# The normed operand h moved by 32 bytes in its SBUF partitions

## The chip, the core and the metric

The kernel runs on one core of a Trainium2 chip. The metric is the device time of one launch in microseconds (us). Below, the SBUF address of a tensor means its byte address within each of the 128 partitions; it is the same in all of them.

## What is computed

The reference passes a 256 x 1024 activation `x` through two blocks of two layers each, all in float32. Cut to what matters here:

```python
for l in range(2):                                # first block
    x = x + 0.5 * swiglu_ffn(rmsnorm(x, ffn1_norm[l]), ffn1_w_up[l], ffn1_w_down[l])
    x = x + mixer(rmsnorm(x, mix_norm[l]), w_in[l], ...)      # windowed attention + 31-tap conv
    x = x + 0.5 * swiglu_ffn(rmsnorm(x, ffn2_norm[l]), ffn2_w_up[l], ffn2_w_down[l])
    x = rmsnorm(x, final_norm[l])
for i in range(2):                                # second block, modulated by c
    h = rms_norm(x, norm_mix_pre[i]) * (1.0 + sc_m) + sh_m
    y = mixer_ab(h, ...) if i == 0 else mixer_c(h, ...)       # recurrence + sparse attention; short conv
    x = x + (1.0 + g_m) * rms_norm(y, norm_mix_post[i])
    h = rms_norm(x, norm_ffn_pre[i]) * (1.0 + sc_f) + sh_f
    y = conv_ffn(h, ...)
    x = x + (1.0 + g_f) * rms_norm(y, norm_ffn_post[i])
```

So nearly all the work is products of a normed activation `h` (1024 channels, 256 tokens) with weight matrices, and, in the four-plus-two feed-forward layers, of a hidden tile with the down projection.

## The kernel before

**Split products.** Every float32 weight and every float32 operand is split in two fp32r parts, a high part and a low one, and each product is made of three matmuls: high x high, high weight x low operand, low weight x high operand. `product` writes them:

```python
mm(o, w_hi[:, n, at], hi, first, False, share=share)
mm(o, w_hi[:, n, at], lo, False, False, share=share)
mm(o, w_lo[:, n, at], hi, False, last, sig, share)
```

The first operand is stationary (128 x 128, put in by a weight load), the second one moves (128 x 256). All matmuls go through the helper on line 522, so all have that line in the profile.

**Weights.** There are 663 weight tiles of 128 x 1024 floats (512 KB). SP's queue loads each into one of six `w_raw` slots; ScalarE copies it to `w_hi` (line 1053), VectorE subtracts to make `w_lo` (line 1477), each in one of three slots. A tile serves 24 matmuls, for eight blocks of 128 along the contraction.

**The operands.** `h_hi` and `h_lo` hold the normed activation as eight blocks of 256 tokens. ScalarE writes `h_hi` (lines 1083, 1097, 1243, 1383) and VectorE `h_lo` (lines 1505, 1567, 1807, 1818, 2079, 2092). They are the moving operand in `column`, `column_pair`, `normed_pair` and `late_pair`, and the stationary one in `token_product` (there a slice of `w_hi` or `w_lo` moves). `hid_hi` and `hid_lo` hold the hidden tile of a feed-forward layer, two buffers each; `spare_operands` holds four more tiles. In `late_pair` and the columns after it, one column's 24 matmuls take `hid` for two blocks, `spare_operands` for two and `h` for four, all added up in the same half of a PSUM bank.

**A feed-forward step** (132 of them, line 1591 on) is two columns of 24 matmuls with `h` moving, into the two halves of a bank, and then the `down` product, 24 matmuls with `hid` moving, each block into another bank half. TensorE's program, and so the order of work, is written out by hand; other engines follow it by semaphores.

**Where the tensors lie.** `sb` reserves SBUF tensors one behind the other, each rounded up to 32 bytes. Addresses in the built programs:

| tensor | bytes | before | after | before, mod 64 | after, mod 64 |
|---|---|---|---|---|---|
| `work` | 8192 | 24704 | 24704 | 0 | 0 |
| `w_hi` | 12288 | 58496 | 58496 | 0 | 0 |
| `w_lo` | 12288 | 70784 | 70784 | 0 | 0 |
| `h_hi` | 8192 | 83072 | 83104 | 0 | 32 |
| `h_lo` | 8192 | 91264 | 91296 | 0 | 32 |
| `vecs` | 5696 | 99456 | 99520 | 0 | 0 |
| `tabs` | 13980 | 105152 | 105216 | 0 | 0 |
| `gate_a` | 2048 | 119136 | 119200 | 32 | 32 |
| `hid_hi` | 2304 | 121184 | 121248 | 32 | 32 |
| `hid_lo` | 2304 | 123488 | 123552 | 32 | 32 |
| `spare_operands` | 4096 | 125792 | 125856 | 32 | 32 |
| `arena` | 78880 | 149952 | 150016 | 0 | 0 |

Every block of `w`, `h`, `hid` and `spare_operands` is a multiple of 512 bytes long, so each block has its tensor's remainder. Before the change `w_hi`, `w_lo`, `h_hi` and `h_lo` lie at multiples of 128 bytes, and `hid_hi`, `hid_lo` and `spare_operands` 96 bytes past one.

Of the kernel before, what the change touches and what calls it, by code (L numbers as in the profile page):

```python
# [193 lines left out]
def build(nc, x_in, weights, vecs_in, tables_in, bv_in, mod_in, out):  # L194
    with ExitStack() as ctx:
        def sb(name, *shape, dt=F32):
            return ctx.enter_context(nc.sbuf_tensor(name, [P, *shape], dt))
# [9 lines left out]
        w_raw = sb("w_raw", RAW, TILE)  # L207
        w_hi = sb("w_hi", SPLIT, TILE, dt=F32R)
        w_lo = sb("w_lo", SPLIT, TILE, dt=F32R)
        h_hi = sb("h_hi", KT, SEQ, dt=F32R)  # L210
        h_lo = sb("h_lo", KT, SEQ, dt=F32R)
        vecs = sb("vecs", N_VEC)
        tabs = sb("tabs", N_TAB)
        gate_a = sb("gate_a", 2, SEQ)
# [2097 lines left out]
```

## Time and profile before

| | |
|---|---|
| time, median of 3 runs | 2372.85 us (2372.59 to 2374.2) |
| time of the profiled execution | 2372.82 us |
| its span, first to last instruction | 2371.0 us |
| mean granted TensorE clock | 0.982 |
| TensorE matmuls | 18598, 98% of the span |
| weight loads | 18598, 95% |
| VectorE | 2844, 73% |
| ScalarE | 1739, 50% |
| HBM read | 403.07 MB, 170 GB/s over the span |

Busy time of a matmul is from its start to its modelled end, and matmuls overlap, so 98% says that the engine always has one in flight, and not how fast they follow each other. That pace is read from the starts in the timeline. The profiled execution took 1.8 us more than its span.

### The profile page before, as it was taken

The page shows a single profiled execution, that of the slowest core. Times are in us where ns is not written, and L with a number is a line of the kernel's source. Part 1 is how long each engine was busy: PE and PEld are TensorE (multiplying, and loading weights), DVE is VectorE, ACT ScalarE, POOL GpSimd, SP SyncE. Part 2 cuts the span into 40 slices and gives each one's busy share as a digit, 9 for nine tenths or more (in the row PEclk, how much of TensorE's full clock was granted, in tenths as well). Part 3 has the DMA queues.
Part 4 walks back from the last instruction along what each step waited for, and adds up shares of the span by engine and source line. Part 5 has one row for each costly group of instructions (what it writes and reads, how often), then busy time and mean ns, then how long its engine had stood idle before and what let it go on. Part 6 is the DMA issues. An engine that isn't in the chain of part 4 may idle for free.

```text
span 2371.0 us, 46678 instructions
## 1 busy us (share of the span) xinstructions
PE 2316.3 (98%) x18598; PEld 2259.9 (95%) x18598; DVE 1731.8 (73%) x2844; ACT 1179.2 (50%) x1739; POOL 98.5 (4%) x196
## 2 busy tenths in 40 slices
PE   8999999999999999999999999999999999999998
PEld 8999999999999999999999999989888999999997
DVE  6667899868667866899976766777445766667766
ACT  4335444565444444554455544446454565435564
POOL 0000020000000000022000000000000000000000
PEclk9999999999999999999999999999699999999999
DMA  8775555235775776565415677443122455353552
GB/s 310 235 242 189 184 167 170 87 126 198 248 243 197 267 239 230 166 182 174 143 55 194 233 238 239 143 151 117 44 72 72 159 180 183 125 169 125 181 182 97
DMA packets 114082, 412.31 MB, mean 174 GB/s; under 512 B 13984, under 2 KB 14112, under 8 KB 113696
## 3 DMA queue, kind: packets, MB, share of 16 engines
q1 hardware_dynamic: 96768, 352.26, 44.5%
q0 software_dynamic: 16896, 56.64, 7.8%
q8 instruction: 94, 1.54, 0.3%
q10 hardware_dynamic: 288, 1.57, 0.2%
q14 instruction: 36, 0.29, 0.0%
HBM read 403.07 MB, written 1.05 MB: 170 GB/s over the span
## 4 chain that ended last, share of the span: by engine, by line
PE 91%; DVE 6%; ACT 2%; issue 1%; DMA 0%; DVEq 0%; SPq 0%; ACTq 0%
PE bank L522 90%; PE bank L707 1%; DVE arena L1680 1%; DVE w_lo L1477 1%; DVE rinv L1513 0%; ACT w_hi L1053 0%; ACT arena L1362 0%; DMA vecs<-vectors 0%; DVE arena L1799 0%; DVE mod_w_buf L1762 0%; DVE arena L2066 0%; DVE work L2055 0%; DVE rinv L1796 0%; DVE mod_w_buf L2048 0%; ACT rinv L1076 0%
## 5 line engine op out<-in xcount | busy, mean ns | idle before, releaser
L522 PE MATMUL bank<-h_hi,w_hi 128*128 128x256 f32 x3840 | 1095.0, 287 | 12.6 <-ACT h_hi L1083 4.0
L522 PE MATMUL bank<-h_hi,w_lo 128*128 128x256 f32 x3840 | 1082.4, 283 | 0.0
L522 PE MATMUL bank<-h_lo,w_hi 128*128 128x256 f32 x3840 | 1069.2, 284 | 0.1
L1477 DVE TENSOR_TENSOR w_lo<-w_raw,w_hi 128x1024 fp32r<-128x1024 f32 x663 | 807.9, 1222 | 335.2 <-ACT w_hi L1053 329.8
L1053 ACT ACTIVATE w_hi<-w_raw 128x1024 fp32r<-128x1024 f32 x663 | 699.6, 1057 | 612.5 <-PE bank L522 611.9
L522 PEld LDWEIGHTS bank<-h_hi,w_hi 128*128 128x128 f32 x3840 | 738.4, 192 | 26.9 <-issue 15.8
L522 PEld LDWEIGHTS bank<-h_hi,w_lo 128*128 128x128 f32 x3840 | 738.6, 192 | 0.0
L522 PEld LDWEIGHTS bank<-h_lo,w_hi 128*128 128x128 f32 x3840 | 729.9, 192 | 3.7 <-DVE h_lo L1505 2.2
L522 PE MATMUL bank<-hid_hi,w_hi 128*128 128x256 f32 (+1 forms) x1168 | 332.8, 285 | 9.8 <-DVE w_lo L1477 2.8
L522 PE MATMUL bank<-hid_lo,w_hi 128*128 128x256 f32 (+1 forms) x1168 | 330.3, 283 | 0.0
L522 PE MATMUL bank<-hid_hi,w_lo 128*128 128x256 f32 (+1 forms) x1168 | 330.0, 283 | 0.0
L522 PEld LDWEIGHTS bank<-hid_hi,w_hi 128*128 128x128 f32 x1168 | 222.7, 191 | 13.2 <-issue 9.4
L522 PEld LDWEIGHTS bank<-hid_hi,w_lo 128*128 128x128 f32 x1168 | 223.5, 191 | 0.0
L522 PEld LDWEIGHTS bank<-hid_lo,w_hi 128*128 128x128 f32 x1168 | 223.3, 191 | 0.0
L1680 DVE SCALAR_TENSOR_TENSOR arena<-arena,vecs 128x256 f32<-128x256 f32 x520 | 215.1, 478 | 0.0
L522 PE MATMUL bank<-arena 128*128 128x64 f32 (+3 forms) x640 | 111.3, 320 | 3.2 <-DVE arena L2002 1.7
L1858 DVE SCALAR_TENSOR_TENSOR mod_w_buf<-mod_w_buf,c_act 128x1024 f32<-128x1024 f32 x84 | 107.5, 1279 | 1.5 <-DMA mod_w_buf<-mod_w 1.2
L1591 DVE TENSOR_TENSOR hid_hi<-gate_a,bank 128x256 fp32r<-128x256 f32 x132 | 55.3, 419 | 69.3 <-ACT gate_a L1130 68.8
L522 PEld LDWEIGHTS bank<-arena 64*128 64x128 f32 (+1 forms) x640 | 92.3, 206 | 12.4 <-DVE work L2031 1.9
L500 POOL DMA_DIRECT2D mod_w_buf<-mod_w x96 | 51.1, 533 | 1072.7 <-DVE mod_w_buf L1858 537.6
L1130 ACT ACTIVATE gate_a<-bank 128x256 f32<-128x256 f32 x88 | 34.0, 386 | 114.4 <-PE bank L522 114.4
L522 PE MATMUL bank<-w_hi,h_hi 128*128 128x256 f32 (+1 forms) x240 | 69.0, 288 | 2.1 <-DVE arena L1751 1.4
(248 smaller groups left out, 2074.2 us busy)
## 6 DMA issues: line engine op xcount, KB each, us to landing
w_raw<-weights SPq DMA_DIRECT2D x663, 512.0 KB, 3.4
mod_w_buf<-mod_w POOLq DMA_DIRECT2D x96, 512.0 KB, 4.8
mod_w_buf<-arena POOLq DMA_DIRECT2D x96, 64.0 KB, 3.6
tabs<-shape_tables SPq DMA_DIRECT2D x1, 1682.0 KB, 14.1
work<-v_bias ACTq DMA_DIRECT2D x2, 768.0 KB, 4.4
x<-x_fm SPq DMA_DIRECT2D x1, 1024.0 KB, 5.1
out_fm<-x SPq DMA_DIRECT2D x4, 256.0 KB, 2.2
vecs<-vectors SPq DMA_DIRECT2D x1, 708.0 KB, 10.5
```

The costliest lines, as they stand in the source:

```text
L500: pool.dma_start(mod_w[:, n % MOD_BUF, :], mod_in[n]).then_inc(mod_w_full[n % MOD_BUF], 16)
L522: ins = pe.matmul(o, lhs, rhs, start=start, stop=stop, skip_group_check=share)
L707: ins = pe.transpose(o, src, tab("identity"))
L1053: act_f(w_hi[:, n % SPLIT, :], w_raw[:, n % RAW, :], ACT.Copy).then_inc(hi_ready, 1)
L1130: act_f(gate_a[:, par, :], half(UP + par, 0), ACT.Silu).then_inc(gate_ready, 1)
L1477: v.tensor_tensor(w_lo[:, n % SPLIT, :], w_raw[:, n % RAW, :], w_hi[:, n % SPLIT, :].bitcast(F32), ALU.subtract).then_inc(lo_ready[n % SPL ...
L1591: v.tensor_tensor(hid_hi[:, par, :], g, half(b, 1), ALU.mult)
L1680: ins = v.scalar_tensor_tensor(dst[:, m, :], src[:, m, k:k + SEQ], tap, dst[:, m, :], ALU.mult, ALU.add)
L1858: ins = v.scalar_tensor_tensor(o, src, c, o, ALU.mult, ALU.add)
```

## The change

Eight floats (32 bytes) are reserved ahead of `h_hi`, and eight behind `h_lo`. Nothing reads or writes them. `h_hi` and `h_lo` move by 32 bytes, and all that is reserved behind them by 64. No instruction is added, taken out or moved on any engine; the two programs differ in the line numbers (by 2 behind the change) and in addresses.

```diff
         w_raw = sb("w_raw", RAW, TILE)
         w_hi = sb("w_hi", SPLIT, TILE, dt=F32R)
         w_lo = sb("w_lo", SPLIT, TILE, dt=F32R)
+        sb("half_line", 8)
         h_hi = sb("h_hi", KT, SEQ, dt=F32R)
         h_lo = sb("h_lo", KT, SEQ, dt=F32R)
+        sb("other_half_line", 8)
         vecs = sb("vecs", N_VEC)
         tabs = sb("tabs", N_TAB)
```

## Rows read from the trace of the kernel before

**Rows 1.** The page: span, busy time (share of span) and instructions of each engine, chain's shares.

```profile
span 2371.0 us, 46678 instructions
PE 2316.3 (98%) x18598; PEld 2259.9 (95%) x18598; DVE 1731.8 (73%) x2844; ACT 1179.2 (50%) x1739; POOL 98.5 (4%) x196
...
PE 91%; DVE 6%; ACT 2%; issue 1%; DMA 0%; DVEq 0%; SPq 0%; ACTq 0%
```

**Rows 2.** Groups of TensorE: count, busy us, mean ns of one, idle us before.

```profile
L522 PE MATMUL bank<-h_hi,w_hi 128*128 128x256 f32 x3840 | 1095.0, 287 | 12.6 <-ACT h_hi L1083 4.0 <-DVE w_lo L1477 3.5 <-DVE h_lo L1567 3.2
L522 PE MATMUL bank<-h_hi,w_lo 128*128 128x256 f32 x3840 | 1082.4, 283 | 0.0
L522 PE MATMUL bank<-h_lo,w_hi 128*128 128x256 f32 x3840 | 1069.2, 284 | 0.1
L522 PE MATMUL bank<-hid_hi,w_hi 128*128 128x256 f32 (+1 forms) x1168 | 332.8, 285 | 9.8 <-DVE w_lo L1477 2.8 <-DVE hid_lo L1928 2.5 <-DVE hid_lo L1594 2.4
...
L522 PE MATMUL bank<-w_hi,h_hi 128*128 128x256 f32 (+1 forms) x240 | 69.0, 288 | 2.1 <-DVE arena L1751 1.4 <-DVE w_lo L1477 0.7
```

**Rows 3.** Tile h_lo on TensorE, 230 to 268 us: ns min/median/max; first, last start.

```profile
L522 PE MATMUL bank<-h_lo,w_hi x106: 283/283/283, 229.8 to 267.6; 128*128 128x256 f32 x106
```

**Rows 4.** Timeline of one feed-forward step on TensorE: start us, us, instruction.

```profile
124.55 0.28 PE L522 MATMUL bank<-h_hi,w_hi 128*128 128x256 f32 x1
...
125.61 0.28 PE L522 MATMUL bank<-h_hi,w_hi 128*128 128x256 f32 x1
...
130.29 0.28 PE L522 MATMUL bank<-hid_hi,w_hi 128*128 128x256 f32 x1
...
130.53 0.28 PE L522 MATMUL bank<-hid_hi,w_lo 128*128 128x256 f32 x1
...
133.14 0.28 PE L522 MATMUL bank<-h_hi,w_hi 128*128 128x256 f32 x1
```

**Rows 5.** Timeline of one column that takes hid, spare_operands and then h.

```profile
542.86 0.28 PE L522 MATMUL bank<-hid_hi,w_hi 128*128 128x256 f32 x1
...
544.28 0.28 PE L522 MATMUL bank<-h_hi,w_hi 128*128 128x256 f32 x1
544.39 0.28 PE L522 MATMUL bank<-h_lo,w_hi 128*128 128x256 f32 x1
...
545.71 0.28 PE L522 MATMUL bank<-hid_hi,w_hi 128*128 128x256 f32 x1
```

**Rows 6.** Tiles hid_lo (130.3 to 133.1 us) and spare_operands (whole span) on TensorE.

```profile
L522 PE MATMUL bank<-hid_lo,w_hi x8: 277/280/285, 130.4 to 132.9; 128*128 128x256 f32 x8
...
L522 PE MATMUL bank<-spare_operands,w_hi x128: 277/281/285, 500.3 to 1299.6; 128*128 128x256 f32 x128
```

**Rows 7.** Groups of VectorE and ScalarE, shapes apart, that write a split part.

```profile
L1594 DVE TENSOR_TENSOR hid_lo<-gate_a,hid_hi 128x256 fp32r<-128x256 f32 x132 | 56.1, 425 | 4.5
...
L1807 DVE TENSOR_TENSOR h_lo<-work,h_hi 128x256 fp32r<-128x256 f32 x16 | 6.1, 422 | 3.6 <-ACT h_hi L1243 3.2
...
L1083 ACT ACTIVATE h_hi<-work 128x256 fp32r<-128x256 f32 x40 | 15.9, 418 | 9.4 <-DVE work L1518 9.4
```

**Rows 8.** Line 1680, the convolution's taps, and line 1277: ns min/median/max.

```profile
L1680 DVE SCALAR_TENSOR_TENSOR arena<-arena,vecs x520: 470/478/487, 241.8 to 2121.6; 128x256 f32<-128x256 f32 x174
...
L1277 ACT ACTIVATE hid_hi<-arena x8: 400/414/419, 1590.8 to 1605.9; 128x256 fp32r<-128x256 f32 x8
```

**Rows 9.** Windows: us, busy (count) of PE, PEld, DVE, ACT, POOL; clock, DMA, GB/s.

```profile
300.00:360.00 60.00, 60.00 (x556) 57.69 (x551) 57.71 (x102) 27.64 (x53) 15.42 (x32) 1.00 0.55 172
360.00:380.00 20.00, 18.93 (x170) 18.05 (x169) 19.40 (x38) 7.75 (x12) 3.06 (x6) 1.00 0.53 175
380.00:408.00 28.00, 28.00 (x224) 27.09 (x223) 28.00 (x53) 10.76 (x13) 0.00 (x0) 1.00 0.56 186
```

**Rows 10.** Cores: span and mean granted TensorE clock.

```profile
core 0: 2371.0 us, clock 0.982
```

## The prediction

> **What bounds the kernel now.** I read the page first. TensorE has a matmul in flight for 98% of the span, and 91% of the chain that ended last is TensorE [rows 1]. The groups of TensorE say which matmuls: three groups of 3840 have `h` moving, 11,520 of 18,598, and their idle time before them is 12.6, 0.0 and 0.1 us [rows 2]. So they hardly wait; the time is their number times the pace at which they follow each other, and the mean duration of 283 to 287 ns is not that pace, since they overlap.
>
> The pace is in the starts. Between 229.8 and 267.6 us there are 106 matmuls of `h_lo`, every third one of an unbroken run: 37.8 us over 105 gaps of three matmuls is 120.0 ns per matmul, and all 106 durations are 283 ns [rows 3]. The stream with `h` moving is locked to one rhythm.
>
> The same trace has matmuls that already lie as the change will put `h`: `hid_hi`, `hid_lo` and `spare_operands` are at 32 mod 64, with the same shape, type and stationary tiles. In a feed-forward step the 22 gaps from 130.53 to 133.14 us, `hid` moving, take 2.61 us, 118.6 ns each; in the same step the 39 gaps from 125.61 to 130.29 us, with `h` moving, take 4.68 us, 120.0 ns [rows 4]. That could come from the bank that `down` changes with each block. The column that takes both kinds excludes it: twelve matmuls of `hid` and `spare_operands` start from 542.86 to 544.28 us, 1.42 us or 118.3 ns each; then, in the same half bank with the same weight tile, come twelve of `h`, of which the last eleven take 545.71 - 544.39 = 1.32 us, 120.0 ns [rows 5]. Durations say the same: `hid_lo` and `spare_operands` spread over 277 to 285 ns with medians of 280 and 281, where `h_lo` has 283 throughout [rows 3, 6]. The position of the moving operand, or where it stands to the weights, is worth about 1.5 ns per matmul. I take 118.5 ns as the pace off a multiple of 64, between 118.3 and 118.6.
>
> **The change part by part.** It adds no instruction and no wait. Five things could change.
>
> *Matmuls with `h` moving.* In the feed-forward layers a gain is already there in part: the first nine matmuls after `hid` still run fast, 124.55 to 125.61 us, 117.8 ns each, before the stream locks [rows 4]. So I cost whole steps. One is 133.14 - 124.55 = 8.59 us for 72 matmuls; at 118.5 ns it would be 8.53. That is 0.06 us, for 132 steps (as many as line 1594 has rows, [rows 7]) 7.9 us. The steps hold 132 x 48 = 6,336 matmuls with `h`; the other 5,184 lose 120.0 - 118.5 = 1.5 ns each, 7.8 us. Together 15.7 us.
>
> *What of it can't be banked.* The mean clock is 0.982 [rows 10]. If that is time at 1.2 in place of 2.4 GHz, (1 - 0.982) x 2 x 2371 = 85 us, 3.6% of the span, ran at the lower level; there a matmul of 256 columns takes about twice as long, and I expect no gain: -0.6 us. And in each of the first block's two mixers VectorE is the tighter engine for a while: busy 57.71 of 60 us, 19.40 of 20 and 28.00 of 28 [rows 9]. A faster TensorE gains nothing where VectorE makes the next `w_lo` late. From 360 to 380 us TensorE has 170 matmuls, of which I take 150 as `h` moving: 150 x 1.5 ns = 0.2 us, twice 0.4 us. From 300 to 360 us there are 60 / 0.120 = 500, so 0.75 us per mixer and 1.5 us in both; VectorE has 2.3 us idle of 60 there, so I count half as lost, 0.8 us. Together -1.2 us. What is late next there is VectorE's own work, the taps and the low parts.
>
> *Matmuls with `h` stationary.* These are 3 x 240 = 720 [rows 2]; `h` moves off and the moving weight slice stays on a multiple of 64. No row shows a stationary operand off such a multiple beside a 256-column fp32r one on it. If what counts is how the two stand to each other, they gain 1.5 ns each, 1.1 us, less the 384 in windows where VectorE is busy all the time (192 per mixer, the third window): 336 x 1.5 = 0.5 us. If only the moving operand counts, nothing. I take 0.3 us and keep -0.7 (1 ns worse each) to +0.5.
>
> *VectorE and ScalarE on `h`.* VectorE writes `hid_lo`, off a multiple of 64, in 425 ns and `h_lo`, on it, in 422; ScalarE writes `hid_hi` in 414 (median) and `h_hi` in 418 [rows 7, 8]. The 31 taps read the same row at starts 4 bytes apart, and all 520 lie between 470 and 487 ns with a median of 478 [rows 8]. So the shift costs these engines nothing: at most 3 ns for each of some 124 writes of `h_lo`, 0.4 us, mostly in the norms where TensorE waits. I take 0.
>
> *All that lies behind `h`, moved by 64 bytes.* Remainders to 64 stay. Remainders to 128 change: `hid` and `spare_operands` go from 96 to 32. Before, the moving operand that is off stands 32 bytes below a multiple of 128, and the weights on one; after, all stand 32 above. No row shows that. I take the pace of 118.5 for both, since both leave 32 when divided by 64; the third rival prices the doubt.
>
> **The sum.** 15.7 - 0.6 - 1.2 + 0.3 = 14.2 us less. The profiled execution took 2372.82 us, 0.03 from the median, so the time is 2372.8 - 14.2 = 2358.6 us, 0.60% less. Its own range: with 118.3 ns and all banked, 132 x (8.59 - 8.52) + 5,184 x 1.7 ns + 0.5 = 9.2 + 8.8 + 0.5 = 18.5 us, 2354; with 118.8 and the same losses doubled, 132 x 0.04 + 5,184 x 1.2 ns - 3.6 - 0.7 = 5.3 + 6.2 - 4.3 = 7.2 us, 2366.
>
> **The rivals.** *Nothing changes.* The spread of `hid` could come from something else that sets it apart, such as its distance from the weights (`h` lies right behind `w_lo`, `hid` 22 KB beyond `h`), or the fast rhythm could be one that falls to 120.0 in runs longer than the 24 matmuls of `down`; the first nine of `h` in a step do run fast and then lock. For it: the change keeps that distance. Against it: in the column of [rows 5] the stream takes up 120.0 one matmul after `h` comes, and 118.6 holds through all of `down`. The time would be 2372.8.
> The Trainium skill speaks for this rival. "TensorE: Matmul & The Clock Gate", Part 2, says of the two read ports that loading the next tile's weights takes no SBUF bandwidth from the running matmul; "SBUF — State Buffer", on Door 1, gives SBUF lines of 16 bytes, to which a shift by 32 changes nothing. By both the time stays at 2372.8. The trace agrees with neither as the whole story, since equal matmuls differ by 1.5 ns with no other difference that I can name than where they lie.
>
> *A bigger gain.* With `h` off, no part of a run falls back to 120.0, and the whole stream could settle at the quick end of what `hid` shows: 277 ns against 283 [rows 6] is 6 ns; half of it on 11,520 matmuls is 34.6 us, 2338. For it: durations do reach it. Against it: the mean pace over 22 matmuls is 118.6, so quick ones are paid for by slow ones.
>
> *Slower.* The place is `product` itself, at the third of these remainders: with every moving operand 32 bytes above the weights' multiple of 128, each matmul could meet the weight load once more, where 32 bytes below it met it less. The slow end of `hid` is 285 ns, 2 ns over `h` [rows 6]: 11,520 x 2 = 23.0 us, and the 3,504 of `hid` [rows 2] would go from 118.5 to 122.0, 12.3 us; together 35 us, 2408. It decides from 120.0 ns on for `h`, if `hid` keeps its pace; if `hid` goes along, all at 119.7 is even (11,520 x 0.3 = 3,504 x 1.2, roughly, without the fast starts). A 256-column operand of 1,024 bytes off a multiple of 64 also touches 17 stretches of 64 bytes and not 16, which would speak for slower; `hid` has that too and is faster.
>
> **How the numbers follow.** The forecast has 0.64, no change 0.14, the bigger gain 0.06, slower 0.16. A measurement of this kernel tells about 0.2%, 4.7 us, from no change. All of the forecast's own range, 2354 to 2366, is beyond that, so faster has 0.64 + 0.06 = 0.70; of the slower case 0.01 is within the bound, which makes same 0.15 and slower 0.15. The range for 8 in 10 takes in the forecast and no change: 2352 to 2375.
>
> **What would show it.** In the changed kernel's trace, a run with only `h` moving such as 230 to 268 us should have starts 118.5 ns apart and durations that spread from 277 to 285 ns; a feed-forward step should take 8.53 us; `h_lo`'s writes and the taps should stay at 422 and 478 ns; VectorE should be busy for all of the token pairs of both first mixers, and these should take as long as before. The forecast is wrong if `h` still runs at 120.0, or if `hid` leaves 118.5.

## The result and the profile after

The changed kernel takes 2342.66 us (median of 4 runs, 2339.43 to 2342.86), the kernel before 2373.11 on the same chip: a ratio of 0.9868, 95% interval [0.9851, 0.9885], so 30 us or 1.3% faster. The forecast was 14.2 us, with a range that ended at 2352. Direction and place were right, and the size was half of what came.

The page of the changed kernel, in the lines that answer to [rows 1]:

```profile
span 2337.6 us, 46678 instructions
PE 2280.9 (98%) x18598; PEld 2222.3 (95%) x18598; DVE 1729.4 (74%) x2844; ACT 1180.0 (50%) x1739; POOL 98.2 (4%) x196
...
PE 91%; DVE 6%; ACT 2%; issue 1%; DMA 0%; DVEq 0%; SPq 0%; ACTq 0%
```

The span, of the fastest of the four runs, is 33.4 us shorter with the same instructions and the same shares in the chain. Its groups of TensorE (count, busy us, mean ns, idle before; compare [rows 2]):

```profile
L524 PE MATMUL bank<-h_hi,w_hi 128*128 128x256 f32 x3840 | 1082.3, 284 | 13.7 <-DVE w_lo L1479 4.0 <-ACT h_hi L1085 4.0 <-DVE h_lo L1569 3.2
L524 PE MATMUL bank<-h_hi,w_lo 128*128 128x256 f32 x3840 | 1069.6, 280 | 0.0
L524 PE MATMUL bank<-h_lo,w_hi 128*128 128x256 f32 x3840 | 1057.7, 281 | 0.1
L524 PE MATMUL bank<-hid_hi,w_hi 128*128 128x256 f32 (+1 forms) x1168 | 329.6, 282 | 10.3 <-DVE w_lo L1479 3.0 <-DVE hid_lo L1930 2.5 <-DVE hid_lo L1596 2.4
```

`h` lost 3 ns in mean duration, and `hid`, which the forecast had as unchanged, lost 3 too (285 to 282). Idle time before each group rose by about 1 us at most: no engine took TensorE's place as the bound. The tile `h_lo` on TensorE between 230 and 268 us (count, ns min/median/max, first and last start; compare [rows 3]):

```profile
L524 PE MATMUL bank<-h_lo,w_hi x108: 277/280/281, 230.0 to 267.9; 128*128 128x256 f32 x108
```

37.9 us over 107 gaps of three is 118.1 ns per matmul, where it was 120.0, and the durations are no longer all alike. Two feed-forward steps from the timeline (start us, us, instruction), the first from the first layer, the second from the layer at 600 us; compare [rows 4]:

```profile
132.02 0.28 PE L524 MATMUL bank<-h_hi,w_hi 128*128 128x256 f32 x1
...
137.67 0.28 PE L524 MATMUL bank<-hid_hi,w_hi 128*128 128x256 f32 x1
...
140.50 0.28 PE L524 MATMUL bank<-h_hi,w_hi 128*128 128x256 f32 x1
...
606.25 0.28 PE L524 MATMUL bank<-h_hi,w_hi 128*128 128x256 f32 x1
...
611.85 0.28 PE L524 MATMUL bank<-hid_hi,w_hi 128*128 128x256 f32 x1
...
614.65 0.28 PE L524 MATMUL bank<-h_hi,w_hi 128*128 128x256 f32 x1
```

The first takes 8.48 us (117.8 ns a matmul), the second 8.40 (116.7): before, every steady step took 8.59. In the second, `h` and `hid` both run at 116.7 ns. About two thirds of the steps of this trace take 8.40 and one third 8.48, each for whole stretches of a layer; that is 132 x 0.16 = 21 us of the 33.4. The other 12 us lie outside the steps. Matched start by start in the two traces, the 5,184 matmuls with `h` there gain 2.9 ns each where they follow without a wait (15 us), and late operands take 3.5 us of it back.

Groups of VectorE and ScalarE, then line 1682 (the taps), and the windows of [rows 9]:

```profile
L1596 DVE TENSOR_TENSOR hid_lo<-gate_a,hid_hi 128x256 fp32r<-128x256 f32 x132 | 56.1, 425 | 4.5
...
L1809 DVE TENSOR_TENSOR h_lo<-work,h_hi 128x256 fp32r<-128x256 f32 x16 | 6.1, 422 | 3.6 <-ACT h_hi L1245 3.2
...
L1085 ACT ACTIVATE h_hi<-work 128x256 fp32r<-128x256 f32 x40 | 15.9, 420 | 9.4 <-DVE work L1520 9.4
...
L1682 DVE SCALAR_TENSOR_TENSOR arena<-arena,vecs x520: 464/477/485, 238.9 to 2091.0; 128x256 f32<-128x256 f32 x174
...
300.00:360.00 60.00, 60.00 (x558) 57.87 (x557) 58.57 (x102) 30.10 (x56) 16.30 (x34) 1.00 0.57 172
360.00:380.00 20.00, 18.82 (x169) 17.86 (x168) 19.74 (x39) 5.46 (x6) 0.47 (x1) 1.00 0.53 180
380.00:408.00 28.00, 28.00 (x226) 26.94 (x224) 28.00 (x55) 13.07 (x18) 0.00 (x0) 1.00 0.51 171
```

The other engines take what they took, and VectorE is as tight as before in the first block's mixers.

### The profile page after: what moved, and what is told of

Its sections match the earlier page's. It is cut to its first block, busy times and chain, and to the rows that moved or that the text cites. A ratio compares the mean times of both kernels' runs of the same rounds, so it can differ in the third digit from the quotient of the medians.

```text
span 2337.6 us, 46678 instructions
## 1 busy us (share of the span) xinstructions
PE 2280.9 (98%) x18598; PEld 2222.3 (95%) x18598; DVE 1729.4 (74%) x2844; ACT 1180.0 (50%) x1739; POOL 98.2 (4%) x196
## 4 chain that ended last, share of the span: by engine, by line
PE 91%; DVE 6%; ACT 2%; issue 1%; DMA 0%; DVEq 0%; SPq 0%; ACTq 0%
PE bank L524 90%; PE bank L709 1%; DVE w_lo L1479 1%; DVE arena L1682 1%; DVE rinv L1515 0%; ACT w_hi L1055 0%; DMA vecs<-vectors 0%; DVE arena L1801 0%; ACT arena L1364 0%; DVE mod_w_buf L1764 0%; DVE arena L2068 0%; DVE rinv L1798 0%; DVE work L2057 0%; ACT rinv L1078 0%; ACT arena L1312 0%
## 5 line engine op out<-in xcount | busy, mean ns | idle before, releaser
L524 PE MATMUL bank<-h_hi,w_hi 128*128 128x256 f32 x3840 | 1082.3, 284 | 13.7 <-DVE w_lo L1479 4.0
L524 PE MATMUL bank<-h_hi,w_lo 128*128 128x256 f32 x3840 | 1069.6, 280 | 0.0
L524 PE MATMUL bank<-h_lo,w_hi 128*128 128x256 f32 x3840 | 1057.7, 281 | 0.1
L524 PEld LDWEIGHTS bank<-h_hi,w_hi 128*128 128x128 f32 x3840 | 725.8, 189 | 28.8 <-issue 17.4
L524 PEld LDWEIGHTS bank<-h_hi,w_lo 128*128 128x128 f32 x3840 | 725.8, 189 | 0.0
L524 PEld LDWEIGHTS bank<-h_lo,w_hi 128*128 128x128 f32 x3840 | 717.2, 189 | 4.6 <-DVE h_lo L1507 2.7
```

The source lines that it names most:

```text
L524: ins = pe.matmul(o, lhs, rhs, start=start, stop=stop, skip_group_check=share)
```

## The experiments

From here on the **distance** of an operand is the address of the moving tensor less that of the weights, modulo 256. Within each tensor the blocks are multiples of 512 bytes apart, and so are `w_hi` and `w_lo`, so each moving tensor has one distance. Before the change `h` has 0, `hid` and `spare_operands` 224; after it all three have 32. In each kernel only reserved bytes differ, unless said otherwise. "Step" is one feed-forward step near 600 us, with the pace of its 48 matmuls with `h` and its 24 with `hid`; starts are read to 0.01 us, so these paces are good to some 0.2 and 0.4 ns. Each run has one trace. Ratios are to the kernel before, with 95% intervals.

| run | h | hid | time, us | ratio | step, us | h ns | hid ns |
|---|---|---|---|---|---|---|---|
| before | 0 | 224 | 2373.11 | 1 | 8.59 | 119.6 | 118.8 |
| changed | 32 | 32 | 2342.66 | 0.9868 [0.9851, 0.9885] | 8.40 | 116.7 | 116.7 |
| e1 | 32 | 96 | 2353.66 | 0.9917 [0.99, 0.9933] | 8.54 | 118.1 | 119.6 |
| e2 | 0 | 32 | 2371.94 | 0.9994 [0.9984, 1.0003] | 8.59 | 120.0 | 117.9 |
| e3 | 64 | 96 | 2355.4 | 0.9926 [0.9909, 0.9942] | 8.54 | 117.9 | 120.0 |
| e4 | 96 | 96 | 2383.49 | 1.0039 [1.0025, 1.0053] | 8.64 | 120.0 | 120.0 |
| e5 (weights and h moved) | 0 | 64 | 2374.02 | 1.0002 [0.9993, 1.0012] | 8.59 | 120.0 | 117.9 |
| e6 (weights by 32, h by 128) | 96 | 64 | 2372.34 | 0.9994 [0.9985, 1.0004] | 8.58 | 120.0 | 117.5 |
| e7 (h_hi 16, h_lo 144) | 16/144 | 224 | 2352.34 | 0.9916 [0.99, 0.9933] | 8.49 | 117.7 | 118.3 |
| e8 (h_hi 32, h_lo 128) | 32/128 | 96 | 2358.58 | 0.9939 [0.9923, 0.9956] | 8.53 | 117.9 | 119.6 |
| e9 (step near 2222 us) | 64 | 64 | 2347.84 | 0.9896 [0.9879, 0.9912] | 8.48 | 117.7 | 117.9 |
| e10 | 32 | 64 | 2333.63 | 0.9829 [0.9812, 0.9845] | 8.33 | 116.9 | 113.3 |
| e11 | 160 | 160 | 2354.77 | 0.9915 [0.9898, 0.9931] | 8.45 | 117.3 | 117.5 |
| e12 (weights moved too) | 32 | 32 | 2340.16 | 0.9862 [0.9846, 0.9879] | 8.48 | 117.9 | 117.5 |
| e13 | 192 | 192 | 2304.46 | 0.9718 [0.9702, 0.9734] | 8.17 | 113.3 | 113.8 |
| e15 (288, 32 to 512) | 32 | 32 | 2339.92 | 0.9858 [0.9841, 0.9874] | 8.40 | 116.7 | 116.7 |
| e16 | 32 | 224 | 2344.81 | 0.9874 [0.9856, 0.9891] | 8.45 | 116.9 | 118.3 |
| e17 | 128 | 128 | 2363.4 | 0.9959 [0.9944, 0.9973] | 8.54 | 118.8 | 118.3 |
| e18 | 224 | 224 | 2358.23 | 0.9937 [0.992, 0.9954] | 8.52 | 118.3 | 118.3 |

Several traces hold steps of more than one length, each for stretches of a layer: 8.40 and 8.48 us in the changed kernel, e12 and e15; 8.47 and 8.53 in e1; 8.33 and 8.43 in e10; 8.45, 8.54 and 8.64 in e11; 8.16 and 8.48 in e9, e13 and e14. The steady steps of the other kernels agree within 0.05 us. The row shows the one near 600 us. A pace that a stretch keeps is called its rhythm below.

**First question: which part of the change gave it?** The expectations of the first runs count remainders to 128 and call 224 "96"; that was too coarse, and e1, e3 and e4 moved `hid` from 224 to 96 without my meaning to (e7 and e8 have the same flaw in `h_lo`, below).

e1 moves `h` by 32 and what lies behind by 128:

```diff
+        sb("pad_before_h", 8)
         h_hi = sb("h_hi", KT, SEQ, dt=F32R)
         h_lo = sb("h_lo", KT, SEQ, dt=F32R)
+        sb("pad_behind_h", 24)
```

> h_hi and h_lo 32 bytes on as in the change, but 96 bytes behind them in place of 32, so that all that lies behind keeps its remainder to 128 (hid and spare_operands 96). Theory A, the remainders to 128 of moving and stationary operand decide together: h runs at 117.0 ns a matmul as after the change, hid goes back to about 118.4 (it had 118.6 before); 3504 matmuls x 1.4 ns = 5 us over the changed kernel, about 2347. Theory B, only being off a multiple of 64 counts and hid ran slower before because it came out of locked runs of h: h and hid both at 117.0, about 2342.

Measured 2353.66 us, 11 more than the changed kernel where theory A had 5: `hid`, now at 96, runs at 119.6 ns and not at 118.4, and `h` at 118.1 where the changed kernel has 116.7. Theory B is out.

e2 leaves `h` and moves all behind it by 64 bytes (`+ sb("pad_behind_h", 16)` behind `h_lo`).

> h stays where it was (a multiple of 128); only what lies behind it moves by 64 bytes, so hid and spare_operands go from remainder 96 to 32. Theory A: h keeps 120.0 ns, hid goes from 118.4 to 117.0, about 2373 - 5 = 2368. Theory B: no remainder to 64 changes, so nothing does: 2373.

Measured 0.9994, no difference. Its timeline shows why theory A's 5 us did not come:

```profile
602.94 0.28 PE L523 MATMUL bank<-h_hi,w_hi 128*128 128x256 f32 x1
...
608.70 0.28 PE L523 MATMUL bank<-hid_hi,w_hi 128*128 128x256 f32 x1
...
611.53 0.28 PE L523 MATMUL bank<-h_hi,w_hi 128*128 128x256 f32 x1
```

`hid` is quicker (2.83 us for 24, where it took 2.85), but the 48 matmuls with `h` now take 5.76 us, 120.0 ns each, where they took 5.74: most of the quick start that they had after `hid` at 224 [rows 4] is gone. The step stays at 8.59 us. So moving the rest is worth nothing alone; beside a moved `h` it counts, as e1 shows.

e3 (`h` by 64) and e4 (`h` by 96), both with what lies behind moved by 128: 16 and 16 floats reserved for e3, 24 and 8 for e4.

> h 64 bytes on: a multiple of 64, not of 128; what lies behind moves by 128 and keeps its remainders. Theory A (remainder to 128): h leaves 120.0 ns for another pace, and I can't say which; hid keeps 118.4. Theory B (remainder to 64): h stays at 120.0, 2373.

> h 96 bytes on (where hid is, 96 mod 128), what lies behind keeps its remainders. Theory A: h runs as hid did before, about 118.5 ns, 1.5 ns less on 11520 matmuls, 2373 - 15 = 2358, which is what the prediction had. Theory B: 117.0 as after the change, 2342.

e3, `h` on a multiple of 64, is 0.7% faster; theory B predicted no change. e4, `h` off it as in the change, is 0.4% slower than the kernel before:

```profile
607.35 0.29 PE L524 MATMUL bank<-h_hi,w_hi 128*128 128x256 f32 x1
...
613.11 0.29 PE L524 MATMUL bank<-hid_hi,w_hi 128*128 128x256 f32 x1
...
615.99 0.29 PE L524 MATMUL bank<-h_hi,w_hi 128*128 128x256 f32 x1
```

All 72 matmuls of the step take 8.64 us, 120.0 ns each. Being on or off a multiple of 64 bytes is not what counts.

**Second question: the operand's own place, or its distance from the weights?** e5 moves weights and `h` by 32; e6 moves the weights by 32 and `h` by 128, so that `h` keeps its remainder to 128 (both edits in one, the remarks are mine):

```diff
+        sb("pad_before_w", 8)
         w_hi = sb("w_hi", SPLIT, TILE, dt=F32R)
         w_lo = sb("w_lo", SPLIT, TILE, dt=F32R)
+        sb("pad_before_h", 24)         # e6 only
         h_hi = sb("h_hi", KT, SEQ, dt=F32R)
         h_lo = sb("h_lo", KT, SEQ, dt=F32R)
+        sb("pad_behind_h", 24)         # e5 only
```

> w_hi, w_lo and h all 32 bytes on (remainder 32 to 128), the rest keeps its remainders (hid 96). Theory R, what counts is where the moving operand stands to the stationary one: h is 0 bytes from the weights again and runs at 120.0 ns, hid stands 64 from them; about 2370. Theory M, what counts is the moving operand's own remainder: h at 117.3 ns as with h alone moved, about 2354.

> only w_hi and w_lo 32 bytes on; h on a multiple of 128 and hid at 96 as before. Theory R: h stands 32 below the weights, as with h at 96, and runs at 120.0 ns with durations that spread; hid stands 64 above, about 117.7 ns; some 5 us either side of 2373. Theory M: h keeps 120.0 ns with all durations alike, hid 118.4, 2373 as before.

In e5 `h` lies where the change put it, 32 off, and runs as in the kernel before: the tile `h_lo`, 230 to 260 us,

```profile
L524 PE MATMUL bank<-h_lo,w_hi x84: 283/283/283, 229.8 to 259.7; 128*128 128x256 f32 x84
```

29.9 us over 83 gaps of three, 120.1 ns, all durations alike, and 1.0002 in time. Weights and `h` both moved against `x`, `work` and `w_raw`, so where they lie against those counts for nothing here. In e6 `h` is on a multiple of 128 as before, and the time of 0.9994 fits both theories. Its durations spread over 281 to 285 ns where they had been 283 throughout, and `hid`, whose remainder to 128 stayed, takes 117.5 ns where it took 118.4, close to e5, which has it at the same distance of 64. `h` takes 120.0 in the steps, which both theories had. e12 moves weights by 32 and the operands by 64, so distance 32 with `h` on a multiple of 64:

> weights at 32, all moving operands at 64, so on a multiple of 64 bytes but 32 from the weights. Theory R (distance to the stationary operand): 2342 as the changed kernel, 116.7 ns. Theory M (the moving operand's own remainder): as with all at 64, 2346 or more; the shifted weights are also written by ScalarE and VectorE, which should cost nothing.

Measured 0.9862, the changed kernel's 0.9868 within both intervals, and its steps take 8.40 or 8.48 us, as there. e5 and e12 decide it and e6 agrees in its paces: the distance counts, and the own remainder to 64 or 128 does not (theory R).

**Third question: finer, and for each part of h?** e7 takes `h_hi` and `h_lo` as slices that begin 4 floats into rooms of 32 floats more; e8 reserves 8 floats ahead of `h_hi` and 24 between the two.

```diff
-        h_hi = sb("h_hi", KT, SEQ, dt=F32R)
-        h_lo = sb("h_lo", KT, SEQ, dt=F32R)
+        h_room = [sb(name, KT * SEQ + 32, dt=F32R)[:, 4:4 + KT * SEQ] for name in ("h_hi", "h_lo")]
+        h_hi, h_lo = (r.rearrange("p (k t) -> p k t", k=KT) for r in h_room)
```

> h_hi and h_lo 16 bytes on, the rest keeps its remainders. If stretches of 16 bytes are what the engine fetches by (the rule that the prediction set beside its first rival), 16 is as good as 32: 117.3 ns and 2354. If the pace follows the distance in finer steps or only in steps of 32, h stands between 0 and 32: 117.3 to 120.0 ns, 2354 to 2373.

> h_hi 32 bytes on, h_lo where it was, the rest keeps its remainders. If each matmul's pace follows its own operand, two of three matmuls run at 117.3 and the third at 120.0 ns, 118.2 on average: about 2373 - 13 = 2360. If the stream locks as a whole, it is 120.0 or 117.3 throughout: 2373 or 2354.

Neither edit does what its expectation says. A room of 32 floats more is 128 bytes, so in e7 `h_hi` has a distance of 16 and `h_lo` one of 144; in e8 the 8 and 24 floats put `h_lo` at 128 and not at 0. To 128 bytes, as I then counted, both were as meant. e7 gives 0.9916, less than e16's 0.9874 with all of `h` at 32 and `hid` also at 224; what 16 bytes alone are worth, no run shows. e8's 2358.58 is near the 2360 that it was expected to have with `h_lo` at 0, but that is luck: nothing lay at 0. Its `h` runs at 117.9 ns, where e1 with all of `h` at 32 has 118.1 or less and e17 with all at 128 has 118.8; whether each matmul follows its own operand is not shown by that.

**Fourth question: how many bytes does the distance count to?** Floats reserved ahead of `h` and behind it: e9 16 and 8, e10 8 and 16, e11 40 and 8, e15 72 and 8, e17 32 and 8, e13 48 and 8.

> h, hid and spare_operands all 64 bytes from the weights (to 128). If the pace follows the distance, all run at the 117.7 ns that h had at 64 with hid at 96: 132 steps x 72 x (119.3 - 117.7) ns + 5184 x 2.3 ns = 27 us less, 2346. If only being off a multiple of 64 gives the full gain, this stays near 2373, or at 2355 as with h at 64 alone.

> h 32 bytes from the weights, hid and spare_operands 64. If what matters is that no operand stands at 0 or 96, about as the changed kernel: 2342 to 2346. If the full gain needs all moving operands at one distance, it stays near 2353, as with hid at 96.

> h, hid and spare_operands 160 bytes from the weights to 256, so 32 to 128. If the distance counts to 128 bytes, 2342 as the changed kernel and 116.7 ns in a feed-forward step; if to 256 or more, another time.

> h 288 bytes from the weights (32 to 256, 288 to 512), hid and spare_operands 32 to 512: both as in the changed kernel to 256, and exchanged to 512. If the distance to 256 decides, 2342 as the changed kernel, 117.0 ns for both; if more than 256 bytes count, another time.

> h, hid and spare_operands 128 bytes from the weights, which fills the gap in the row 0, 32, 64, 96, 160, 192, 224. If 128 is to the two streams what 0 is, 120.0 ns and about 2383; if the good distances are 64 and 192 and the row has a period of 128 in the main, 120.0 as well; if 0 alone locks at 120.0, about 118 ns and 2350.

32 and 160 differ (0.9868 and 0.9915, disjoint intervals), and so do 96 and 224 (1.0039 and 0.9937; every steady step takes 8.64 and 8.52 us): 128 bytes are too few. 32 and 288 agree (0.9868 and 0.9858): 256 do, as far as these runs go. 128 is neither as 0 nor as 64; its 0.9959 was in none of my expectations. e10 beat its expectation of 2342 to 2346 by 8 us.

> h, hid and spare_operands 192 bytes above the weights (to 256), that is 64 below. So far, by the distance to 256: 0 gave 120.0 ns a matmul, 16 117.8, 32 117.0, 64 117.7, 96 119.9, 160 117.9, 224 118.4, and the 240 full-width token products, where the weights move 192 above h, 116.1. If the distance to 256 decides, about 117 ns and 2343 to 2355. If the distance to 128 did, 117.7 as at 64, 2348.

At 192 the kernel takes 2304.46 us, 2.8% less than before and 1.6% less than the changed one, and no expectation of mine had it. `h` lies on a multiple of 64 there. A step:

```profile
572.91 0.28 PE L524 MATMUL bank<-h_hi,w_hi 128*128 128x256 f32 x1
...
578.35 0.28 PE L524 MATMUL bank<-hid_hi,w_hi 128*128 128x256 f32 x1
...
581.08 0.28 PE L524 MATMUL bank<-h_hi,w_hi 128*128 128x256 f32 x1
```

8.17 us, 113.5 ns a matmul. This is the fastest version found. Its four times spread from 2298.9 to 2309.52 us, and the trace is that of the fastest.

**Fifth question: was the forecast's proxy sound?** e16 gives `h` 32 and keeps `hid` at 224 (8 floats ahead, 56 behind); e18 puts `h` at `hid`'s 224 (56 and 8).

> the change's part on h alone, done cleanly: h 32 bytes from the weights, all that lies behind moved by 256, so that hid and spare_operands keep the distance of 224 to 256 that they had before (in the earlier run with h at 32 they went from 224 to 96). If each operand's pace follows its own distance to 256, h at 117.0 to 117.3 and hid at 118.4 ns: 3504 x 1.4 ns = 5 us over the changed kernel, 2347. If hid at 224 was only fast in the wake of h at 0, hid at 119.6 and 2353.

> h 224 bytes from the weights, just where hid stood before, and hid and spare_operands kept at 224. This is the kernel that the prediction's proxy speaks of. If the pace belongs to the distance, all moving operands run at 118.4 ns as hid did: 132 x (8.59 - 8.52) us + 5184 x 1.6 ns = 17 us less, 2356, the time that the prediction gave. If hid's 118.4 was only had next to h at 0, 120.0 and 2383, as with all at 96.

e16: 2344.81, expected 2347. e18: 2358.23, expected 2356. Its step:

```profile
601.20 0.28 PE L524 MATMUL bank<-h_hi,w_hi 128*128 128x256 f32 x1
...
606.88 0.28 PE L524 MATMUL bank<-hid_hi,w_hi 128*128 128x256 f32 x1
...
609.72 0.28 PE L524 MATMUL bank<-h_hi,w_hi 128*128 128x256 f32 x1
```

118.3 ns for both kinds, as `hid` had before [rows 4]. The pace belonged to the distance of 224.

**Sixth question: does a distance have one pace?** In e9 every steady step takes 8.48 us, except in one layer, near 1840 us, where all take 8.16:

```profile
1840.38 0.28 PE L524 MATMUL bank<-h_hi,w_hi 128*128 128x256 f32 x1
...
1848.54 0.28 PE L524 MATMUL bank<-h_hi,w_hi 128*128 128x256 f32 x1
...
2222.36 0.28 PE L524 MATMUL bank<-h_hi,w_hi 128*128 128x256 f32 x1
...
2230.84 0.28 PE L524 MATMUL bank<-h_hi,w_hi 128*128 128x256 f32 x1
```

e14 is e9 with one small matmul more per layer, whose result nothing reads:

```diff
                 down(0, 0)
+                release, state["release"] = state["release"], False
+                mm(bank[6][:, SEQ:SEQ + 64], tab("mean_all"), tab("mean_all")[:, 0:64])
+                state["release"] = release
                 t0, p0 = state["tile"], state["pair"]
```

> h, hid and spare_operands at 64 as in the run before, and in each feed-forward layer one more matmul of 128 x 64 (0.1 us, into a free half bank) ahead of the steady loop. There, with the same addresses, five of the six layers ran all their steps in 8.48 us (117.8 ns) and one all of them in 8.16 us (113.3 ns). If the rhythm depends on how the stream enters it, layers change sides: each that goes to 8.16 us gains 6 us. If it follows from the addresses alone, the step times stay as they are, and the time at 2348 + 0.6.

```profile
1844.69 0.28 PE L524 MATMUL bank<-h_hi,w_hi 128*128 128x256 f32 x1
...
1853.17 0.28 PE L524 MATMUL bank<-h_hi,w_hi 128*128 128x256 f32 x1
...
2220.68 0.28 PE L524 MATMUL bank<-h_hi,w_hi 128*128 128x256 f32 x1
...
2228.84 0.28 PE L524 MATMUL bank<-h_hi,w_hi 128*128 128x256 f32 x1
```

The two layers changed sides: 8.48 us in the one that had 8.16, and 8.16 in the last, which had 8.48 (and in the first part of one layer of the first block). So the addresses alone do not fix the rhythm. That the added matmul made the layers change sides is not shown: there is one trace of each kernel, and the executions of e14 spread from 2333.01 to 2353.02 us, so a layer may well fall differently from one execution to the next. The time, 2336.49 us with a ratio of 0.986 [0.9817, 0.9904], overlaps e9's.

The trace of e13 shows the change happen. Its first layer begins at 8.16 us a step; then TensorE waits once for a `w_lo`, and the steps that follow in this stretch take 8.48:

```profile
36.74 0.28 PE L524 MATMUL bank<-h_hi,w_hi 128*128 128x256 f32 x1
...
44.90 0.28 PE L524 MATMUL bank<-h_hi,w_hi 128*128 128x256 f32 x1
...
50.82 0.39 PE L524 MATMUL bank<-hid_hi,w_hi 128*128 128x256 f32 x1 [0.32 <-DVE w_lo L1479]
...
53.75 0.28 PE L524 MATMUL bank<-h_hi,w_hi 128*128 128x256 f32 x1
...
62.23 0.28 PE L524 MATMUL bank<-h_hi,w_hi 128*128 128x256 f32 x1
```

All other steady steps of e13 take 8.16 us. So 64 and 192 share both lengths, and most of the 43 us between e9 and e13 go with which of them the stretches hold; why 192 holds the quick one so much more often is not known.

## Why the prediction was wrong in size

**That TensorE's pace sets the time: right.** The span fell with the pace, and no wait took its place: TensorE's idle time before these groups grew by 1.6 us.

**That `hid` stands as a proxy for `h` off a multiple of 64: the step that failed.** The forecast measured 118.5 ns on matmuls with a distance of 224 and wrote of the new distance, 32, "I take the pace of 118.5 for both, since both leave 32 when divided by 64". e4 and e5 show that the remainder to 64 carries nothing (off it at 120.0 ns in both), e12 and e13 that an operand on a multiple of 64 can have the full gain or more. The prediction did name the distance from the weights, in its first rival, but as near or far (22 KB), and wrote that the change keeps it; to 256 bytes it takes `h` from 0 to 32 and `hid` from 224 to 32. The proxy itself was measured well: the kernel that really puts `h` at 224, e18, takes 2358.23 us, where the forecast said 2358.6.

**That `hid` keeps its pace: wrong by the same step.** It was moved from 224 to 32 by the 64 bytes behind `h`, and went from 118.4 to 116.7 or 117.8. e16 leaves it at 224 and costs 2 us against the changed kernel, where 5 were expected; the two intervals overlap, so of the change's 30 us some 28 come with `h` alone moved. e2 shows the same 64 bytes worth nothing while `h` stays at 0.

**The term of the moving `h`: 15.7 us forecast, 31 found before waits.** Steps fell from 8.59 to 8.40 or 8.48 and not to 8.53 us (21 us with `hid`'s part, against 7.9), and the other 5,184 matmuls by 2.9 ns and not 1.5 where nothing waits (15 us against 7.8). Start by start, some 27 us of the 33.4 come between matmuls with `h`, waits and all, 5 with `hid`.

**What can't be banked: right in place, too small.** The forecast took off 1.2 us for late operands; between the starts of matmuls with `h`, 22 waits are new and others longer, 3.5 us together. VectorE is busy for all of the token windows again, and the serial piece in front of them, from ScalarE's `w_hi` at 367.73 us to TensorE's next matmul at 378.61 us before, lasts 10.88 us in both traces. The idle time that the profile puts down to `w_lo` grew by only 0.7 us (7.1 to 7.8). No run here separates the 0.6 us for the lower clock.

**Matmuls with `h` stationary: +0.3 us forecast, some 0.6 found.** Here the weights move, and go from distance 0 to 224 from `h`. 21 gaps before, then 21 after:

```profile
362.72 0.28 PE L522 MATMUL bank<-w_lo,h_hi 128*128 128x256 f32 x1
...
365.24 0.28 PE L522 MATMUL bank<-w_lo,h_hi 128*128 128x256 f32 x1
...
358.09 0.28 PE L524 MATMUL bank<-w_lo,h_hi 128*128 128x256 f32 x1
...
360.58 0.28 PE L524 MATMUL bank<-w_lo,h_hi 128*128 128x256 f32 x1
```

They go from 120.0 to 118.6 ns. The prediction had this as what follows "if what counts is how the two stand to each other".

**VectorE and ScalarE on `h`: right.** 422 and 425 ns on VectorE as before, 420 for 418 on ScalarE, the taps 477 for 478.

**The rivals.** The bigger gain, at 0.06 and 2338 us, was nearest to what came; I argued against it with the mean of 118.6, which was another distance's mean. "Slower" had the right place, the third remainder, and the wrong sign here, but it is what happens at 96 (e4). "No change" had two rules of the Trainium skill behind it. "TensorE: Matmul & The Clock Gate", Part 2, has the next weight load take no bandwidth from the running matmul. The pace nonetheless goes from 120.0 to 113.3 ns in kernels that differ in nothing but addresses (before, e13). "SBUF — State Buffer", on Door 1, gives lines of 16 bytes. If nothing else counted, e7, which moves `h` by whole multiples of 16 bytes, would have changed nothing, and it took 21 us off.

**What stays open.** That the running matmul and the next weight load meet in SBUF fits all of this, but no run here separates the two streams, so it was only argued. Distances between those tried are not known, 16 for all of `h` among them. Which rhythm a layer falls into was not predicted by anything here, nor how far it differs between executions, and an operand's pace depends on its neighbour's distance too.

## What to carry to other kernels

When a trace offers a proxy for a changed layout, write down every relation in which it stands (here its distance from the other operand, to 256 bytes), and not only the one that the change is named after; a proxy holds only where all that may count is equal. In a stream of full matmuls that each load new weights, the pace between starts, read off the timeline over some dozen matmuls, is worth more than the busy share, which said 98% at 120.0 ns and 97% at 113.3; read it in several layers, since one set of addresses can hold two paces. Where such a stream is the bound, a few reserved bytes between the stationary and the moving tensors are a cheap size to sweep: here 0 to 224 bytes spanned 2304 to 2383 us.

## What the runs showed of the hardware that I had not expected

- 128x256 fp32r matmuls with their own weight loads follow each other every 113.3 to 120.0 ns where the granted clock is 1.00, by the distance between moving and stationary operand and by the rhythm that the stream is in.
- All operands at one distance: 32 gives 2342.66 us, 64 2347.84, 96 2383.49, 128 2363.4, 160 2354.77, 192 2304.46, 224 2358.23.
- One distance can have two rhythms: 117.8 and 113.3 ns at 64 (e9), each held for a whole layer, and the same two at 192 (e13), where the slow one set in after TensorE had waited 0.32 us for a `w_lo`.
- A neighbour's distance changes the pace of `h`: at 0 it ran its first nine matmuls at 117.8 ns after `hid` at 224, and after `hid` at 32 all 48 of a step take 120.0 on average. `hid` at 64 takes 117.9 ns beside `h` at 0 (e5) and 113.3 beside `h` at 32 (e10).
